# Moving eight value quads of the sample's attention from the retention steps into the first eight attention units

## What is computed

```python
x = LN1(ALPHA * x + 0.5 * SwiGLU_1(x))
x = LN2(ALPHA * x + concat(attention(x), silu(g) * groupnorm(retention(x))) @ w_out)
x = LN3(ALPHA * x + 0.5 * SwiGLU_2(x))
```

```python
# sample attention: 2048 past keys of each sequence lie in 16 pages of 128, found by a page table
att = softmax(where(picked, q @ k_pages.T, -inf)) @ v_pages        # 8 sequences x 4 queries x 8 heads
# retention, for each chunk of 128 prompt tokens
out = ((q @ k.T) * decay) @ v + (q @ state) * xi
state = exp(128 * lg) * state + (k * zeta).T @ v
# the same for the sample's 4 tokens, with a state of its own for each sequence (read, changed, written out)
```

## Time and profile before

| | |
|---|---|
| median of 3 runs | 1536.35 us (1535.57 to 1538.89) |
| the profiled execution: its own time, its span | 1543.76 us, 1542.1 us |
| mean granted TensorE clock of that execution | 0.958 |
| TensorE, VectorE, ScalarE, GpSimd busy | 1444.4, 555.5, 417.4, 193.3 us |

### The profile page before, as it was taken

One profiled execution on the slowest core, in us unless ns is written; L12 is line 12 of the kernel. 1 busy time (PEld: TensorE's weight loads), 2 busy tenths in 40 slices (PEclk: granted clock), 3 DMA queues, 4 the chain that ended last, 5 costly groups with the idle time before them and its releaser, 6 DMA issues. The chain is left out here.

```text
span 1542.1 us, 27205 instructions
## 1 busy us (share of the span) xinstructions
PE 1444.4 (94%) x10150; PEld 1232.9 (80%) x10150; DVE 555.5 (36%) x1102; ACT 417.4 (27%) x622; POOL 193.3 (13%) x309
## 2 busy tenths in 40 slices
PE   6999999999999999999998768799899999999995
PEld 6999999999976567777753226567689999999994
DVE  3333333222241368970203224553533333332224
ACT  3333333212142310000311000242453433422223
POOL 0000000134123011222024210000510000000011
PEclk9999999999999899999999985699999999999998
DMA  5222222233214238787357761301022222223231
GB/s 192 84 82 82 87 90 82 75 109 111 89 61 130 63 122 256 249 265 241 132 192 239 225 198 41 130 1 42 14 78 86 82 95 82 89 71 89 88 85 58
DMA packets 65349, 176.74 MB, mean 115 GB/s; under 512 B 9681, under 2 KB 13778, under 8 KB 65042
## 3 DMA queue, kind: packets, MB, share of 16 engines
q1 hardware_dynamic: 49874, 131.30, 26.7%
q0 software_dynamic: 14560, 40.96, 8.5%
q10 hardware_dynamic: 864, 3.80, 0.6%
HBM read 169.00 MB, written 7.02 MB: 114 GB/s over the span
## 5 line engine op out<-in xcount | busy, mean ns | idle before, releaser
L355 PE MATMUL ps<-x_high,w_high 128*128 128x280 f32 (+1 forms) x1408 | 413.7, 294 | 18.1 <-DVE x_low L1060 10.6
L355 PE MATMUL ps<-x_high,w_low 128*128 128x280 f32 (+1 forms) x1408 | 411.1, 292 | 0.0
L355 PE MATMUL ps<-x_low,w_high 128*128 128x280 f32 (+1 forms) x1408 | 411.0, 292 | 0.0
L1054 DVE TENSOR_TENSOR w_low<-wring,w_high 128x1024 fp32r<-128x1024 f32 (+1 forms) x136 | 163.1, 1200 | 508.4 <-ACT w_high L824 508.3
L355 PEld LDWEIGHTS ps<-x_high,w_high 128*128 128x128 f32 x1408 | 267.9, 190 | 23.0 <-issue 13.6
L355 PEld LDWEIGHTS ps<-x_low,w_high 128*128 128x128 f32 x1408 | 268.0, 190 | 0.0
L355 PEld LDWEIGHTS ps<-x_high,w_low 128*128 128x128 f32 x1408 | 267.5, 190 | 0.0
L355 PE MATMUL ps<-xbuf,wring 128*128 128x280 f32 x1056 | 265.2, 408 | 1.2 <-ACT aux L824 0.9
L824 ACT ACTIVATE w_high<-wring 128x1024 fp32r<-128x1024 f32 (+1 forms) x136 | 140.7, 1035 | 423.6 <-PE ps L355 422.6
L355 PEld LDWEIGHTS ps<-xbuf,wring 128*128 128x128 f32 x1056 | 199.2, 192 | 59.4 <-issue 11.0
L355 PE MATMUL ps<-h_high,w_low 128*128 128x280 f32 (+1 forms) x704 | 203.8, 289 | 0.0
(11 more groups left out here) (176 smaller groups left out, 1246.1 us busy)
## 6 DMA issues: line engine op xcount, KB each, us to landing
wring<-in_wg SPq DMA_DIRECT2D x44, 512.0 KB, 3.5
wring<-in_wu SPq DMA_DIRECT2D x44, 512.0 KB, 3.5
wring<-in_w_in SPq DMA_DIRECT2D x33, 512.0 KB, 4.3
wring<-in_wd SPq DMA_DIRECT2D x32, 512.0 KB, 3.6
dring<-in_k_pool POOLq DMA_DIRECT2D x64, 256.0 KB, 3.7
dring<-in_k_pool SPq DMA_DIRECT2D x64, 256.0 KB, 3.4
dring<-in_v_pool POOLq DMA_DIRECT2D x64, 256.0 KB, 4.1
dring<-in_v_pool SPq DMA_DIRECT2D x64, 256.0 KB, 4.1
```

The source lines that it names most:

```text
L355: return nc.tensor.matmul(out, lhs, rhs, start=start, stop=stop, **kw)
L1054: v.tensor_tensor(wl[:, to, 0:n], w4[:, s, 0:n], wh[:, to, 0:n].bitcast(F32), ALU.subtract) \
```

## The change

`QUADS` goes and `HELD = 8` comes. The last eight quads (pages 8 to 15 of group 1) leave the retention steps. A step calls `value_pages(1)` twice, so it takes two quads; the sample's step takes the one that is left of the first 24. Quad 24 + `u` is taken in attention unit `u`, for `u` from 0 to 7, behind its retention part.

What is moved with them: ScalarE copies group 1's result out in its loop after unit 8, VectorE reduces it after unit 10 and copies it into `mix` after unit 13, TensorE turns it in unit 12 (into bank 7). Only group 0's result is handled ahead of the units. Bank 7 is taken until then, so the units' values use bank 6 alone, and a unit's values wait for the copy of the unit before.

The ring now holds quads while the states are worked on, so states 3 to 6 move into the space of group 0's probabilities (`lg2[:, 0]`), state 7 and `so_b[0]` into the space of the fourth weight (`wring`). They are loaded as soon as group 0 is closed. ScalarE waits for all state writes ahead of its first turned probabilities, which share that space; one of the two buffers for these moves into `scr`, which grows by 64 columns. SP issues its loads in a new order, and output weights 4 to 7 wait until the slots that they cover are free.

```diff
-QUADS = 3
+HELD = 8
...
-        l_b = [scr[:, at:at + 2 * PL].rearrange("p (h n) -> p h n", h=2) for at in (1216, 2272, 3328)]
-        pt_b = [lg2[:, j, 640:1920].rearrange("p (h n) -> p h n", h=2) for j in range(2)]
+        l_b = [scr[:, at:at + 2 * PL].rearrange("p (h n) -> p h n", h=2) for at in (1280, 2336, 3392)]
+        pt_b = [b.rearrange("p (h n) -> p h n", h=2) for b in (lg2[:, 0, 640:1920], scr[:, 0:1280])]
...
-        so_b = [lg2[:, g, 0:512] for g in range(2)]
-        so_rows = [lg2[:, g, 512:576] for g in range(2)]
+        so_b = [wring[:, 3584:4096], lg2[:, 1, 0:512]]
+        so_rows = [aux[:, 2568 + 64 * g:2632 + 64 * g] for g in range(2)]
...
-            return st[:, b, :] if b < 3 else kv[:, b - 3, :]
+            return st[:, b, :] if b < 3 else lg2[:, 0, (b - 3) * 512:(b - 2) * 512] if b < 7 else wring[:, 3072:3584]
...
-            for g in range(2):
-                value_quads(sp, g, 0, kvf)
+            value_quads(sp, 0, 0, kvf)
+            value_quad(sp, 1, 0, kvf)
+            sp.wait_ge(sem("so_full"), 1)
+            sp.wait_ge(sem("w_free3"), OUT_W[3])
             for b in range(3, NB):
-                sp.wait_ge(sem(f"kv_free{b - 3}"), 2 * NPAGE)
-                sp.dma_start(kv[:, b - 3, :], state[b]).then_inc(sem(f"st_in{b}"), 16)
+                sp.dma_start(st_ap(b), state[b]).then_inc(sem(f"st_in{b}"), 16)
+            for pg in range(2, NPAGE - HELD + 2, 2):
+                value_quad(sp, 1, pg, kvf)
             sp.wait_ge(sem("dst_full"), NB)
-            for s in range(4):
+            for s in range(3):
                 weight(s, w_out[s])
+            value_quad(sp, 1, 10, kvf)
+            sp.wait_ge(sem("so_att"), 1)
             sp.wait_ge(sem("st_out"), 16 * NB)
+            weight(3, w_out[3])
+            for pg in (12, 14):
+                value_quad(sp, 1, pg, kvf)
             for d in range(4, KT):
+                if d % 2 == 0:
+                    for s in range(4):
+                        sp.wait_ge(sem(f"kv_free{2 * d - 8 + s}"), 2 * NPAGE)
                 sp.dma_start(out_weight(d), w_out[d]).then_inc(sem(f"wo_in{d}"), 16)
...
-                value_pages(QUADS)
+                value_pages(1)
                 pe.wait_ge(sem("it_done"), t + 1)
...
-                value_pages(QUADS)
+                value_pages(1)
                 ret_out(t)
...
-            value_pages(2 * NPAGE)
+            value_pages(2 * NPAGE - HELD - done[0])
...
-                pt_, bank = pt_b[u % 2], 6 + u % 2
+                pt_ = pt_b[u % 2]
                 pe.wait_ge(sem("apt_done"), u + 1)
-                if u >= 2:
-                    pe.wait_ge(sem("ao_done"), u - 1)
+                if u:
+                    pe.wait_ge(sem("ao_done"), u)
...
-            pe.wait_ge(sem("so_done"), 4)
+            pe.wait_ge(sem("so_done"), 2)
             for u in range(len(pairs) + 1):
...
                     ret_part(u)
+                    value_pages(1)
+                if u == HELD + 4:
+                    sample_turned(1)
...
+                if u == 1:
+                    act.wait_ge(sem("st_out"), 16 * NB)
                 if u >= 1:
                     turned(u - 1, *pairs[u - 1])
+                if u == HELD + 1:
+                    act.wait_ge(sem("so_full"), 2)
+                    ev(so_b[1], ps[:, 7, :]).then_inc(sem("so_out"), 1)
...
+            sample_rows(0)
+            sample_out(0)
...
                     scaled(u, *pairs[u])
+                if u == HELD + 2:
+                    sample_rows(1)
+                if u == HELD + 5:
+                    sample_out(1)
...
-            value_quads(pool, 1, 1, kvf)
+            for pg in range(1, NPAGE - HELD, 2):
+                value_quad(pool, 1, pg, kvf)
...
                 pool.dma_start(rs_o[b], st_ap(b)).then_inc(sem("st_out"), 16)
+            for pg in range(NPAGE - HELD + 1, NPAGE, 2):
+                value_quad(pool, 1, pg, kvf)
```

More of the change, by code:

```diff
@@ L113, in build @@
         scr_at = nc.sbuf_base
-        scr = sb("scr", 4384)
+        scr = sb("scr", 4448)
         cst = sb("cst", CONST_W)
@@ L725, in _, with sample_turned @@
             pe.wait_ge(sem("st_new"), NB)
-            for g in range(2):
+            def sample_turned(g):
                 pe.wait_ge(sem("so_att"), g + 1)
-                tr(ps[0:64, 3, g * P:(g + 1) * P], so_rows[g], 0, P).then_inc(sem("so_turned"), 1)
+                tr(ps[0:64, 7 if g else 3, 0:P], so_rows[g], 0, P).then_inc(sem("so_turned"), 1)
+            sample_turned(0)
             pairs = [(hp, t) for hp in range(4) for t in TILES]
@@ L762, in values @@
             def values(u, hp, t):
-                pt_, bank = pt_b[u % 2], 6 + u % 2
+                pt_ = pt_b[u % 2]
                 pe.wait_ge(sem("apt_done"), u + 1)
-                if u >= 2:
-                    pe.wait_ge(sem("ao_done"), u - 1)
+                if u:
+                    pe.wait_ge(sem("ao_done"), u)
                 for j in range(-1, t + 1):
                     for h in range(2):
-                        o, hc = ps[64 * h:64 * h + 64, bank, 0:P], slice((2 * hp + h) * AD, (2 * hp + h + 1) * AD)
+                        o, hc = ps[64 * h:64 * h + 64, 6, 0:P], slice((2 * hp + h) * AD, (2 * hp + h + 1) * AD)
                         if j < 0:
@@ L801, in _ @@
             pe.wait_ge(sem("ao_done"), len(pairs))
+            pe.wait_ge(sem("so_done"), 4)
             for d in range(KT):
@@ L1002, in _ @@
                     ev(so_b[0], ps[:, 4, :]).then_inc(sem("so_out"), 1)
-                    act.wait_ge(sem("so_full"), 2)
-                    ev(so_b[1], ps[:, 7, :]).then_inc(sem("so_out"), 1)
             pairs = [(hp, t) for hp in range(4) for t in TILES]
@@ L1348, in _, with sample_rows @@
             gated(4, SMP, NS, 0)
-            for g in range(2):
+            def sample_rows(g):
                 dve.wait_ge(sem("so_out"), g + 1)
@@ L1355, in _, with sample_out @@
                 v.reduce_sum(so_rows[g], so_b[g].rearrange("p (h d) -> p d h", h=AH), axis=AX.X).then_inc(sem("so_att"), 1)
-            for g in range(2):
-                dve.wait_ge(sem("so_turned"), 2)
-                t = ps[0:64, 3, g * P:(g + 1) * P].rearrange("p (b a two q) -> p a b two q", b=4, two=2, q=NQ)
+            def sample_out(g):
+                dve.wait_ge(sem("so_turned"), g + 1)
+                t = ps[0:64, 7 if g else 3, 0:P].rearrange("p (b a two q) -> p a b two q", b=4, two=2, q=NQ)
                 for h2 in range(2):
@@ L1400, in out @@
                 dve.wait_ge(sem("ao_full"), u + 1)
-                v.tensor_copy(mix[:, hp, real(t):real(t) + P], ps[:, 6 + u % 2, 0:P]).then_inc(sem("ao_done"), 1)
+                v.tensor_copy(mix[:, hp, real(t):real(t) + P], ps[:, 6, 0:P]).then_inc(sem("ao_done"), 1)
             n = len(pairs)
```

## The result

The changed kernel takes 1493.47 us in the median of 4 runs (1491.85 to 1494.94), the kernel before 1537.62: a ratio of 0.9717, 95% interval 0.9696 to 0.9737. (The three runs of before that the forecast starts from had a median of 1536.35; these are four.) The profiled execution took 1494.77 us, with a span of 1492.0.

The account below looks back on a forecast made before the run. TensorE, busy 94% of the span, was taken as the bound, with retention steps long from waits for value pages. Steps -37.0, sample's step +2.0, hand-over -1.8, attention +10.3 sum to -26.5 us: 1536.35 to 1509.9, range 1499 to 1522.

Parts of the forecast that it names:

- The steps: Four retention steps, two quads each instead of up to six: 97.6 us before, 60.6 after, a gain of 37.0 us.
- step 0: First retention step: still waits for quad 15, which closes group 0, and ends 17.1 us after its start.
- the later ones: The three retention steps after the first: 14.5 us each, the clock falling once and returning in the first half.
- two bounds: Length of a later retention step: 11.6 us at full clock, 17.2 us at half clock throughout.
- the stretch from 870 to 874: Profile row in the retention steps, cited for a clock at half after 4 us with TensorE nearly idle.
- The sample's step: Takes the 24th quad ahead of its cross matmuls: +2.0 us at half clock, +1.0 at full.
- The hand-over: From state stage to attention: only one group handled ahead, first scores and logits earlier, gain 1.8 us (0 to 2.6).
- Queues: Loads on SP and POOL and ScalarE's wait for state writes: all covered, no cost; held quads have 11.9 us against 8.3.
- The attention units: Eight held quads, closing matmuls and a transpose land wholly on TensorE's path: +10.3 us (9.3 at full clock, 18.6 at half).
- The state stage itself: Matmuls with the eight states, after the sample's step: same matmuls and VectorE work, so taken as unchanged.
- full clock everywhere: Lower end of the range, 1499 us, a change of -37.2; the rival with full clock in every step had chance 0.11.
- half clock through a whole step: Rival for the retention steps, from the skill's rule: 17.2 us per later step, sum -18.4, 1518 us; chance 0.13.

Follow-up runs that it names:

- Run 6: Changed kernel plus 128x128x512 matmuls nobody reads where TensorE waits for VectorE's chain: under each step's chain, behind the state stage, ahead of the transpose; 1486.87 us.
- run 7: Changed kernel with each of the eight held quads' matmuls run twice in the attention units, same loads; 1503.36 us.
- run 9: Changed kernel with the 24th quad behind the state stage instead of ahead of it, same work and loads; 1506.63 us.
- run 2: Kernel before, with the last quad (31) left to the sample's step ahead of its cross matmuls, nothing held for the units; 1522.61 us.
- run 3: Kernel before plus three 128x128x512 matmuls nobody reads, ahead of the sample's cross matmuls; 1524.99 us against 1536.42 on the same chip.
- run 10: Changed kernel with the 24th quad behind the state stage and three 128x128x512 matmuls nobody reads in its old place; 1496.22 us.
- run 1: Changed kernel with the 24th quad taken under retention step 3's chain instead of ahead of the sample's cross matmuls; 1504.08 us.
- run 4: Kernel before with QUADS = 2 instead of 3: four quads in each retention step, one left for the sample's step, nothing held; 1504.57 us.
- run 11: Kernel before with QUADS = 2 plus matmuls nobody reads under step 3's chain, behind the state stage and ahead of the sample's transposes; 1499.81 us.

## Why the prediction was wrong

**Right in kind and nearly in size.** The steps: 60.6 us forecast, 57.5 measured; step 0 16.4 for 17.1, the later ones 13.7 for 14.5. The 14.5 was taken near the middle of two bounds and not added up, so its nearness is partly luck. The mechanism is the forecast one: pages are no longer waited for, the chain is, and the clock falls once in each step and comes back in its first half. Four stretches around steps 1 and 2 show it, with the columns of the earlier trace rows:

```profile
844.20:847.50 3.30, 0.00 (x0) 0.00 (x0) 2.79 (x14) 0.30 (x1) 0.00 (x0) 0.83 0.99 345
847.60:853.00 5.40, 4.42 (x20) 3.44 (x24) 2.03 (x4) 0.00 (x0) 0.00 (x0) 0.50 0.48 159
853.80:857.70 3.90, 3.90 (x36) 2.91 (x32) 0.84 (x2) 0.00 (x0) 1.38 (x3) 1.00 0.29 70
857.80:861.40 3.60, 0.00 (x0) 0.00 (x0) 3.09 (x14) 0.30 (x1) 0.70 (x2) 0.81 0.96 284
```

TensorE idles under the chain and the clock falls; the turned keys and the start of the first quad run at half; the output matmuls run at full; then the next chain. Run 6 puts the clock's price at 2 us a step, in the two steps that it held at full. One row was cited for more than it shows: the stretch from 870 to 874 itself reads 1.00, and the fall comes behind it, at 0.50 from 876 to 878.

The sample's step: +2.0 forecast, +2.35 measured. The hand-over: -1.8, measured -1.6. Queues: the list of TensorE's waits over the units names no page and no output weight, as forecast.

**Mis-sized.** The attention units: +10.3 forecast, +8.0 measured. The quads are 1.0 us each, as run 7 confirms; but the clock came back 5.4 us after the first scores (at 924.9) and not 7.7, so unit 0's quad ran at full clock (-1.0 us) and its retention part took 3.36 us instead of 3.99. That is 1.6 of the 2.3 us; the rest is not traced, nor is why the clock came back sooner.

**The step that failed** is the sentence "The state stage itself is as before: same matmuls, same VectorE work". The work is the same; the clock is not. It measured -15.0 us where 0 stood, and by itself it carries the time out of the range: the other stages sum to -31.4, which would have given 1506. The rows to see it were there. The earlier trace rows show 37 us at clock 0.50 in which TensorE was busy for 34.9, and the change sets a quad, a stretch of full work, right ahead of that stage. The stage should have been bounded from both sides, at 0.50 and at 1.00, with a rival for the second. The range's lower end is called full clock everywhere, but it too leaves this stage at half; with the 15 us it would have been 1484. Instead the clock was argued through for the steps, where it was worth 6 us, and taken as given where it was worth 15.

The Trainium skill, TensorE: Matmul & The Clock Gate, section "HAM oscillation — how this bites in real kernels", describes a kernel in which each burst of matmuls starts cold, after a wait for a DMA. The trace agrees, here for a wait on VectorE: after 3.7 us of idle time each later step began at 0.50. What the prediction drew from it, half clock through a whole step, didn't hold; the section of the Trainium skill tells of bursts shorter than the waits between them, and here each later step has some 9 us of matmuls and 3.7 us of idle time under the chain. The Trainium skill, the same page, Part 1, section "What's actually happening", says that throttled is the default and that activity releases it. Here the state stage, in which the profile shows TensorE busy throughout, did not release it in 32.6 us (before) or 32.5 (run 9), while a quad or the added 128x128x512 matmuls ahead of them did (runs 2, 3, 10); once full, it stayed full through the same 17.5 us of work.

**What stays open.** Why one quad brings the clock back, to judge by the times, in all of the changed kernel's eight executions but in eight of ten of run 2's. In runs 1, 2 and 4 the long executions were not profiled. Their lower mean granted clock shows that they lost clock, but not where; that it was in the state stage is argued from run 9's time and from run 11.

## What to carry to other kernels

Read the granted clock of each stage beside its busy share: the time of a stage that is fully busy at half clock can depend on what runs just ahead of it, as here, so price it at both levels whenever a change moves work across its border. Where a chain on another engine leaves TensorE idle, matmuls for nothing, sized to fit inside the wait, can pay for themselves (8.6 us here), but only where nothing late stands ahead of them in the queue. And before building a mechanism that holds work back, try spreading it evenly: here one constant gave 29 of the 40 us in the steps.

## What the runs showed of the hardware

Two levels of one program: with the same instructions, run 1's executions lie at 1493 to 1495 or at 1513 to 1514 us and nothing between, and run 4's likewise. And a full clock survived broken work: over step 3's chain in run 1, with TensorE busy 5.8 of 10.6 us in pieces of about a microsecond, it stayed at 1.00.
